# A hybrid decoder step on one core: the second output gate's weights as eight pieces of 128 columns in place of four slots split by halves

## The reference

```python
h = rmsnorm(x, g_pre1) * (1.0 + sc1) + sh1                 # sc1, sh1, ... from silu(c) @ w_ada
proj = jnp.dot(h, w_in)                                    # 1024 x 5632
hq, hf, hi, hg, aq, ak, av, ua, ub = jnp.split(proj, splits, axis=-1)
o_a = ...   # gated linear recurrence over hq, hf, hi (4 heads), normed and gated by hg
o_b = moba_attend(q, k_all, v_all, pos)    # 8 heads; the 8 sequences read 2048 cached keys and values each
merged = jax.nn.sigmoid(ua) * jnp.dot(o_a, w_proj_a) + jax.nn.sigmoid(ub) * jnp.dot(o_b, w_proj_b)
x = x + gt1 * rmsnorm(jnp.dot(merged, w_out), g_post1)
...         # then a SwiGLU block with w_gu and w_down
```

## Time and profile before

| what | value |
|---|---|
| median of 3 runs | 754.27 us (753.85 to 757.11) |
| profiled execution | 758.49 us, its span 756.7 us |
| TensorE matmul busy | 650.0 us (86% of the span) |
| VectorE, ScalarE, GpSimd busy | 396.1, 274.3, 88.1 us |
| moved by DMA | 168.94 MB, mean 223 GB/s |

### The profile page before, as it was taken

One profiled execution on the slowest core, in us unless ns is written; L12 is line 12 of the kernel. 1 busy time (PEld: TensorE's weight loads), 2 busy tenths in 40 slices (PEclk: granted clock), 3 DMA queues, 4 the chain that ended last, 5 costly groups with the idle time before them and its releaser, 6 DMA issues.

```text
span 756.7 us, 13015 instructions
## 1 busy us (share of the span) xinstructions
PE 650.0 (86%) x5219; PEld 545.0 (72%) x5219; DVE 396.1 (52%) x490; ACT 274.3 (36%) x391; POOL 88.1 (12%) x86
## 2 busy tenths in 40 slices
PE   4759999997696864789998759996999999999996
PEld 1238898875585753587333329985999999999996
DVE  0551475456684555676586325758635453543522
ACT  1232526355122211246312122344645454532421
POOL 2040001203647402000000000001100000000001
PEclk9859999998987989799978969998999999999988
DMA  9895947779577385987999999450465546445201
GB/s 339 318 347 194 352 170 240 244 276 360 163 285 261 129 294 197 385 238 253 332 337 324 317 342 278 154 180 1 137 197 155 173 133 191 145 152 181 91 1 63
DMA packets 98355, 168.94 MB, mean 223 GB/s; under 512 B 6449, under 2 KB 41961, under 8 KB 95106
## 3 DMA queue, kind: packets, MB, share of 16 engines
q1 hardware_dynamic: 92434, 162.85, 63.1%
q10 hardware_dynamic: 5152, 3.08, 1.4%
q0 software_dynamic: 720, 2.32, 0.8%
HBM read 163.51 MB, written 4.72 MB: 222 GB/s over the span
## 4 chain that ended last, share of the span: by engine, by line
PE 63%; DMA 11%; SPq 8%; DVE 8%; issue 3%; POOL 3%; ACT 3%; POOLq 0%; DVEq 0%; ACTq 0%
PE ps L1456 17%; PE ps L1457 16%; PE ps L1458 16%; SPq L313 6%; DMA ring<-cache_k 4%; DMA ring<-w_in 4%; DVE KT L1116 2%; SPq L307 2%; DMA ring<-w_ada 2%; PE ps L1623 2%; POOL wk_lo L495 2%; PE ps L1467 2%; DMA ring<-cache_v 1%; PE ps L1847 1%; PE ps L1676 1%
## 5 line engine op out<-in xcount | busy, mean ns | idle before, releaser
L949 DVE TENSOR_TENSOR w_lo<-ring,w_hi 128x1024 fp32r<-128x1024 f32 (+1 forms) x112 | 134.4, 1226 | 123.2 <-ACT w_hi L567 123.1
L1456 PE MATMUL ps<-h_hi,w_hi 128*128 128x288 f32 x576 | 173.9, 302 | 11.4 <-POOL h_lo L448 6.4
L1457 PE MATMUL ps<-h_lo,w_hi 128*128 128x288 f32 x576 | 172.0, 299 | 0.0
L1458 PE MATMUL ps<-h_hi,w_lo 128*128 128x288 f32 x576 | 171.4, 298 | 0.0
L567 ACT ACTIVATE w_hi<-ring 128x1024 fp32r<-128x1024 f32 (+1 forms) x112 | 113.7, 1039 | 146.6 <-PE ps L1458 90.1
L1456 PEld LDWEIGHTS ps<-h_hi,w_hi 128*128 128x128 f32 x576 | 109.9, 191 | 18.7 <-issue 15.2
L1458 PEld LDWEIGHTS ps<-h_hi,w_lo 128*128 128x128 f32 x576 | 110.4, 192 | 0.0
L1457 PEld LDWEIGHTS ps<-h_lo,w_hi 128*128 128x128 f32 x576 | 110.1, 191 | 0.1
L1116 DVE STREAM_TRANSPOSE KT<-ring 128x2048 f32<-128x2048 f32 x32 | 73.5, 2302 | 44.9 <-DMA ring<-cache_k 38.5
L1623 PE MATMUL ps<-KT,Wk 128*32 128x128 f32 x1024 | 39.3, 302 | 41.4 <-DVE KT L1116 41.4
L1623 PEld LDWEIGHTS ps<-KT,Wk 128*32 128x32 f32 x1024 | 29.7, 120 | 51.0 <-DVE KT L1116 38.6
(11 more groups left out here) (322 smaller groups left out, 1075.1 us busy)
## 6 DMA issues: line engine op xcount, KB each, us to landing
ring<-cache_k SPq DMA_DIRECT2D x128, 256.0 KB, 4.5
ring<-cache_v SPq DMA_DIRECT2D x128, 256.0 KB, 3.9
ring<-w_ada SPq DMA_DIRECT2D x24, 1024.0 KB, 7.7
ring<-w_in SPq DMA_DIRECT2D x22, 1024.0 KB, 7.6
ring<-w_gu SPq DMA_DIRECT2D x44, 512.0 KB, 4.6
ring<-w_down SPq DMA_DIRECT2D x10, 1024.0 KB, 5.0
ring<-w_out SPq DMA_DIRECT2D x4, 1024.0 KB, 7.1
S<-state_hgrn SPq DMA_DIRECT2D x4, 512.0 KB, 7.7
```

The costliest lines, as they stand in the source:

```text
L949: dve.tensor_tensor(w_lo[:, par, k, :], slot4(s)[:, k, :], w_hi[:, par, k, :].bitcast(F32), ALU.subtract).then_inc(sem("lo_split"), 1)
L1456: pe.matmul(dst, h, x_hi, start=first, stop=False)
L1457: pe.matmul(dst, h, x_lo, start=False, stop=False)
L1458: return pe.matmul(dst, l, x_hi, start=False, stop=last)
```

## The change

The columns of `ub` are loaded as eight pieces of 128 columns by 1024 rows, 512 KB each, one behind each of the units 3, 6, ..., 24. A piece is split as a whole: one `hi_k(i)`, one `lo_k(i)`, and its slot is free with `lo_k(i)`. `dense_k(i)` makes all 8 row tiles of one column tile, at the same places as before (behind units 6, 9, ..., 27). The split buffers keep their size (1024 elements per partition). The copies of the result out of PSUM (`evac_k`) become one for each piece. The order of ScalarE's and GpSimd's programs is rewritten around this. As the ring's period is now three units and a piece, all pieces fall into the same slot and the units into the other three.

```diff
 for u in range(NKU):
     RING.append(("key", u))
-    if u in (5, 11, 17, 23):
-        RING.append(("in", WK[u // 6]))
+    if u % 3 == 0 and 3 <= u <= 24:
+        RING.append(("piece", u // 3 - 1))
...
+                elif kind == "piece":
+                    sp.wait_ge(sem("lo_split"), 4 * NF + i + 1)
...
+                elif kind == "piece":
+                    slot_free(n)
+                    sp.dma_start(piece(n), w_src("w_in", 0, 9 * BC + P * i, rows=D, width=P)).then_inc(sem(f"w_landed{n % NSLOT}"), 16)
...
 GpSimd:
+            def lo_k(i):
+                pool.wait_ge(sem("hi_split"), 4 * NF + i + 1)
+                pool.tensor_tensor(wk_lo[:, :, :], piece(N_OF["piece", i]), wk_hi[:, :, :].bitcast(F32), ALU.subtract).then_inc(sem("lo_split"), 1)
...
-            lo_k(14, 0)
-            lo_k(14, 1)
+            lo_k(0)
+            for b in range(4, NSEQ):
+                queries(b)
+            lo_k(1)
             diff(2)
-            queries(4)
-            queries(5)
-            queries(6)
-            queries(7)
             scale_level(2)
             diff(3)
+            lo_k(2)
             scale_level(3)
-            lo_k(15, 0)
-            lo_k(15, 1)
             diff(4)
             scale_level(4)
+            lo_k(3)
             diff(5)
             scale_level(5)
             diff(6)
+            lo_k(4)
             scale_level(6)
-            for w in (16, 17):
-                lo_k(w, 0)
-                lo_k(w, 1)
+            for i in range(5, NPC):
+                lo_k(i)
...
 ScalarE:
+            def hi_k(i):
+                n = N_OF["piece", i]
+                act.wait_ge(sem(f"w_landed{n % NSLOT}"), 16 * in_slot(n))
+                act.wait_ge(sem("w_used"), 4 * NF + i)
+                act.activation(wk_hi[:, :, :], piece(n), ACT.Copy).then_inc(sem("hi_split"), 1)
+            def evac_k(i):
+                act.wait_ge(sem("w_used"), 4 * NF + i + 1)
+                act.activation(proj[:, UB + i, :], ps[:, 4 + i % 2, 0:T], ACT.Copy).then_inc(sem("tile_out"), 1)
...
             raw_scores(0); scores(0)
-            hi_k(14, 0); hi_k(14, 1)
+            hi_k(0); hi_k(1); evac_k(0)
             raw_scores(1); scores(1); level_exp(2)
-            evac_k(14)
+            hi_k(2); evac_k(1)
             level_exp(3); raw_scores(2)
-            hi_k(15, 0)
             scores(2)
-            hi_k(15, 1)
             level_exp(4)
+            hi_k(3); evac_k(2)
             level_exp(5); raw_scores(3)
-            evac_k(15)
             scores(3)
+            hi_k(4); evac_k(3)
             level_exp(6)
-            hi_k(16, 0); hi_k(16, 1)
+            hi_k(5); evac_k(4)
             raw_scores(4); scores(4)
...
 TensorE:
+            def dense_k(i):
+                pe.wait_ge(sem("lo_split"), 4 * NF + i + 1)
+                if i >= 2:
+                    pe.wait_ge(sem("tile_out"), 4 * NF + i - 1)
+                for kt in range(DT):
+                    ins = three(ps[:, 4 + i % 2, 0:T], (wk_hi[:, kt, :], wk_lo[:, kt, :]), h_hi[:, kt, :], h_lo[:, kt, :], kt == 0, kt == DT - 1)
+                ins.then_inc(sem("w_used"), 1)
```

More of the change, by code:

```diff
@@ L257, in build @@
     NF = 7
-    WK, WL = range(14, 18), range(18, 22)
+    NPC, WL = 8, range(18, 22)
     NKU = NVU = 4 * NSEQ
@@ L283, in build, with piece @@
     N_OF = {r: n for n, r in enumerate(RING)}
-    assert B0 == 110 and NA == 38
+    BW = B0 - 22
+    assert BW % NSLOT == 0
     def in_slot(n):
-        pages = RING[n][0] in ("key", "value")
-        return sum((RING[m][0] in ("key", "value")) == pages for m in range(n % NSLOT, n + 1, NSLOT))
+        pages = ("key", "value")
+        kinds = pages if RING[n][0] in pages else ("ada", "in", "piece")
+        return sum(RING[m][0] in kinds for m in range(n % NSLOT, n + 1, NSLOT))
     def w_src(name, row, col, rows=BK * P, width=BC):
         return inp[name][0, bass.ds(row, rows), bass.ds(col, width)].rearrange("(k p) n -> p k n", p=P)
-    def slot8(s):
-        return ring[:, s, :].rearrange("p (k n) -> p k n", n=256)
+    def piece(n):
+        return ring[:, n % NSLOT, 0:DT * P].rearrange("p (k n) -> p k n", n=P)
     def slot4(s):
@@ L341, in load_in @@
                 slot_free(n)
[L342 to L347, removed]
+                g = GROUPS[w // 2] if w < 2 * NF else 7 + (w - WL[0]) // 2
+                sp.dma_start(slot4(n % NSLOT), w_src("w_in", w % 2 * BK * P, g * BC)).then_inc(sem(f"w_landed{n % NSLOT}"), 16)
             for n in range(NA):
@@ L405, in _ @@
             for k in range(2):
-                load_gu(n - NSLOT - 88 + 1, n % NSLOT, 0, k)
+                load_gu(n - NSLOT - BW + 1, n % NSLOT, 0, k)
                 n += 1
@@ L614, in evac_tile @@
                 if j < 3:
-                    act.wait_ge(sem("tile_done"), g * 3 + (j + 1) + (len(WK) if late else 0))
+                    act.wait_ge(sem("tile_done"), g * 3 + (j + 1))
                 else:
-                    act.wait_ge(sem("w_used"), 4 * g + 4 + (2 * len(WK) if late else 0))
+                    act.wait_ge(sem("w_used"), 4 * g + 4 + (NPC if late else 0))
                 b, to = (3 + j, UA + 4 * (g - NF) + j) if late else (j, GROUPS[g] * 4 + j)
@@ L705, in _ @@
             scores(0)
-            hi_k(14, 0)
-            hi_k(14, 1)
+            hi_k(0)
+            hi_k(1)
+            evac_k(0)
             raw_scores(1)
@@ L811, in hi_b @@
             def hi_b(w, rows=BK):
-                n = w + 88
+                n = w + BW
                 s = n % NSLOT
-                before = sum(kind in ("ada", "in") for kind, _ in RING[s::NSLOT]) + (2 if w >= 52 else 0)
-                hi(w, "w_landed", s, 16 * (before + (n - (B0 if w < 52 else 52 + 88)) // NSLOT + 1), w % 2, rows)
+                before = sum(kind in ("ada", "in", "piece") for kind, _ in RING[s::NSLOT]) + (2 if w >= 52 else 0)
+                hi(w, "w_landed", s, 16 * (before + (n - (B0 if w < 52 else 52 + BW)) // NSLOT + 1), w % 2, rows)
             act.wait_ge(sem("oa_ready"), HH)
@@ L1302, in lo_b @@
             def lo_b(w, rows=BK):
-                lo(w, (w + 88) % NSLOT, w % 2, rows)
+                lo(w, (w + BW) % NSLOT, w % 2, rows)
             def gated(cg, j):
@@ L1782, in _ @@
             for i in range(8):
-                between.setdefault(6 + 3 * i, []).append(lambda i=i: dense_k(14 + i // 2, i % 2))
+                between.setdefault(6 + 3 * i, []).append(lambda i=i: dense_k(i))
             for u in range(NKU):
```

34 lines of the change are left out of this document (18 added, 16 removed).

## The result

The changed kernel takes 751.95 us, the median of 17 runs (746.53 to 759.39); the kernel before, in as many runs beside it, takes 758.3 (753.85 to 763.59). The ratio is 0.9915 with a 95% interval of 0.9887 to 0.9943, so 6.4 us or 0.85% are won. (The longest run, 759.39 us, fell in a slower state of the chip, and the ratio leaves it out.) The forecast was 15 us: the sign is right, the size less than half.

What follows compares the result with a forecast made beforehand. It took a loop through SP's wait for the split to bound the key stage, not transfer rate or TensorE. Loops of 25.7 against 31.6 us save 17.7, less 2.8, together 15: 754.27 becomes 739.3 us, range 728 to 752.

Steps and rivals of the forecast that it cites:

- Rival 2: Key stage: the split falls behind its own piece's matmuls, loops stop overlapping; 10 us slower, 764 us; chance 0.11.
- Rival 3: Key stage: transfers alone bound it, last unit transposed at 280 us; 32 us won, 722 us; chance 0.10.
- the loop's third term: Key-stage loop: two more units after the landing, at the transfers' 2.72 us each; 5.4 us.
- 3.6 to SP free: Key-stage loop, first term: from the matmuls' end, upper part 1.07, lower part 2.37 and three hand-overs; 3.6 us.
- 7.4 to the landing: Key-stage loop, second term: SP free to the unit's landing, 6.0 us plus 1.4 (0.5 to 2.3) for the piece ahead.
- the forecast's extra 2.8 at the scores' copy: On ScalarE, upper part 4 waits behind scores(3) for unit 16 and its restrip; 2.8 us lost on one loop.
- the last term: Key-stage loop: last landing to the matmuls' end, through transposition, unit, gram and matmuls; 9.3 us, between 8.6 and 11.
- the wait moved from three units to four: SP's queue: distance from a piece's matmuls to the wait grows by one unit; loop of 25.7 us against 31.6.
- 5.9 us a loop: Key stage: gain claimed for each of three loops of six units, 17.7 us less in all.
- Rival 1: Key stage: restarts come more often, at the lower clock, loop 30.8 us with late lower parts; 2 won, 752; chance 0.13.
- the instructions at nothing: ScalarE, GpSimd and TensorE: instructions stay the same in number and size, so cost nothing by themselves.
- The 747 us that the forecast worked out by the rule: Weight loads: about 2 us fixed cost for each of four more transfers would give back 8 us; not adopted.

Runs made afterwards that it cites:

- experiment 11: The changed kernel with the pieces two units later, behind 5, 8, ..., 26: 725.04 us, 0.9553 of the kernel before.
- experiment 14: The changed kernel with pieces two units later and VectorE's mask copies behind the odd units: 718.03 us, 0.9474 of the kernel before.
- experiment 9: The changed kernel with upper part 4 and the copy of tile 3 ahead of scores(3) on ScalarE: 749.85 us, 0.9886 of the kernel before.
- experiment 12: The kernel before with four 1 MB entries, hi_k/lo_k(16, 0) ahead of level_exp(6)/scale_level(6), and mask copies behind the odd units: 752.55 us, 0.9923.
- experiment 1: The changed kernel with VectorE's mask copies (keep) behind odd units 7 to 21, not even 6 to 20: 745.51 us, 0.9844 of the kernel before.
- experiment 7: The changed kernel with 36 unread extra matmuls on TensorE ahead of each of units 7, 13, 19 and 25: 751.14 us, 0.9888 of the kernel before.
- experiment 13: The changed kernel with mask copies behind the odd units and 36 extra matmuls ahead of units 7, 13, 19, 25: 744.69 us, 0.9827 of before.
- (5): The kernel before with the third entry's first-half upper part ahead of level_exp(6) and lower part ahead of scale_level(6): 752.57 us, 0.9928.
- (6): The changed kernel with hi_k(4) put back behind level_exp(6) and lo_k(4) behind scale_level(6): 753.42 us, 0.9920 of the kernel before.
- experiment 4: The changed kernel's ScalarE, GpSimd and TensorE programs with four 1 MB entries behind units 5, 11, 17, 23: 751.77 us, 0.9920 of the kernel before.
- experiment 2: The changed kernel with the pieces one unit later, behind 4, 7, ..., 25: 734.16 us, 0.9658 of the kernel before.

## Why the forecast was right and where it failed

**Right: the bound.** A loop through SP's wait for the split sets the stage; taking the pieces out wins 32 us, moving the wait by one unit 18 and by two 27. Rival 2 (slower) did not happen. Rival 3 (transfers alone) did not happen in the changed kernel; its end of the stage, 280, is reached with pieces only in experiments 11 and 14. What the stage wins passes through the values' stage: 4.2 us at its end, 4.6 at 514 us. It need not always: the profile of experiment 9 ends the stage 7.4 us before the changed kernel's and starts the last stage only 2.7 us before it.

**Wrong: the loop's third term.** The forecast had, from the end of a piece's matmuls (D), 3.6 to SP free, 7.4 to the landing, 5.4 for two more units, and 9.3 from there to D. Read from the trace after, for the three loops that start at units 7, 13 and 19:
- D to SP free: 3.6, 6.1, 3.6 (the 6.1 is the forecast's extra 2.8 at the scores' copy, here 2.5).
- SP free to landing: 8.6, 8.2, 7.8, a mean of 8.2 for 7.4, within the bounds of 0.5 to 2.3 for the piece.
- Landing to the transposition two units later: 8.7, 9.3, 10.1, a mean of 9.4 for 5.4.
- From there to D: 8.6, 10.0, 6.8, a mean of 8.5 for 9.3.

With the 0.9 of the scores' copy the forecast's loop is 26.6, and the measured one 30.5; 4.0 are missing in the third term and 0.8 in the landing, and the last term gives 0.8 back. The third term was added up as if the next two units came at the transfers' pace. In truth VectorE, in its own order, waits for the gram behind the first unit, copies a mask, and only then transposes the third. `keep` was named nowhere in the working, though it was in the timeline of before; there it costs nothing (experiment 12). With the copies moved the term is 6.0, 6.8 and 6.0 us, and experiment 1 gives back 6.4 us of the 8.6 that were missing. The lower clock lengthens the same wait: the unit and the gram behind each restart take 1.93 and 3.1 to 3.7 us, against 1.08 and 2.05. The forecast allowed for that in the last term, of which it took 9.3 of 8.6 to 11. What it costs by itself stays open; filler that raised the clock in part changed no time (experiments 7 and 13).

**Not shown: that the wait moved from three units to four shortens the loop.** The periods between the restarts, from one profile of each kernel:

| kernel | periods of six units, us | stage ends |
|---|---|---|
| before | 29.8, 35.9, 29.1 | 317.4 |
| changed | 29.6, 33.6, 28.4 | 313.2 |
| before, order swapped (5) | 31.0, 31.5, 29.2 | 310.5 |
| changed, order undone (6) | 28.9, 36.5, 28.7 | 315.5 |

With the old order at unit 18 the changed kernel has the periods of the kernel before, to within 0.9 us. In these profiles the third term took away again what the fourth unit gave to SP's wait. Of the 3.3 us by which the three periods together are shorter in the changed kernel, 2.3 lie in the middle one, which the swap alone shortens by 4.4. Single profiles can differ by 2 us in one period (experiment 9), so this says that no gain of 5.9 us a loop is there, not that there is none.

**Rival 1 came nearest in its numbers, in part by luck.** It put the loop at 30.8 us (measured 30.5) and the gain at 2 us (measured 6.4). Its lower clock behind the restarts is in the trace after; the earlier trace rows, which it names for every dry stretch of before, show 0.50 in one such place (183 to 187 us) and 1.00 in another (283 to 287). But it needed lower parts 2.5 us late, and SP was free 3.6 us after D in two of three loops; the mask copy was not in it.

**Wrong: the instructions at nothing and the orders at a cost of 2.8.** The rewritten order of ScalarE and GpSimd was costed only where it adds a wait. It also takes one away: the level ahead of the lower part at unit 18, which made the period of 35.9 us. In an average of 31.6 it was not seen. That swap alone gives 0.72%, and the pieces without it 0.80%, so the measured 6.4 us can't be split between the two; in the single profiles the swap alone ends the stage at 310.5, the pieces without it at 315.5, both at 313.2. What the pieces alone are worth, 2 us by the stage in one profile or 6 by the times, stays open. Of the 5.9 us that the forecast won in each of three loops, 1.1 remained.

**The rule on transfer size.** The Trainium skill ("DMA: Bandwidth & Descriptors", Bandwidth) advises transfers of 1 MiB or more; its rates were measured on loads issued from GpSimd. By that, four transfers of 1 MB would be ahead of eight of 512 KB. Here they are level (experiment 4 and the changed kernel), and with the mask copies moved the changed kernel leads by 0.8% (experiments 1 and 12). The 747 us that the forecast worked out by the rule mean 7 us won, next to the 6.4 measured, but that is luck: what was missing lies in the third term, and the kernel with four entries is not the faster one. That the size of the entry counts by when its slot comes free fits experiments 2 and 11, and is not separated from the rest.

## What to carry to other kernels

A wait that is moved along an in-order queue is worth what the whole loop through it is worth, so write down every instruction that stands in program order on each engine between the landing and the event that frees the next slot, the small ones too (moving a mask copy of 1.3 us that waits for TensorE shortened the loop by 2.8 us). Before tuning what is split, move where it is queued: the same pieces two units later won 27 us more, four times what the change itself won. And look at periods one by one: a mean of three hid the one that a swap on two engines could mend.

## What was not expected of the hardware

Filler matmuls raised the granted clock from 0.86 to 0.96 over 90 us and changed the time by less than the noise. The Trainium skill ("TensorE: Matmul & The Clock Gate", Part 1) says that the array is at half rate after idling and that activity releases it; the units' 1.94 and 1.08 us agree. In the trace the time so won at one restart was lost at the next wait, where TensorE was found at the lower clock again (1.93 and 3.71 us for unit 15 and its gram in experiment 7).
